# Where the rows that TensorE streams and the ring of weights begin in SBUF: another placement modulo 128 bytes in a hybrid SSD and attention layer

## The reference, cut to what matters

```
proj = x @ w_in                                        # gates | z | xBC | dt | q_a | kv_a
SSD:  conv(width 4) + SiLU on xBC, Mamba-2 scan (32 heads, 8 groups, state 128), y * silu(z), RMSNorm, @ w_ssm_proj
MLA:  q = RMSNorm(q_a) @ w_q_b, latent keys, chunk-causal softmax attention (16 heads), @ w_mla_proj
mix = (sigmoid(g_ssm) * y_ssm + sigmoid(g_mla) * y_mla) @ w_out
h = LN1(ALPHA * x + mix)
y = LN2(ALPHA * h + relu(h @ w_up)**2 @ w_down)        # w_up 1024 x 4096, w_down 4096 x 1024
```

## The kernel before

| operand | start of row k before | start of row k with the change |
|---|---|---|
| `whi`, `wlo` blocks (512 bytes each) | 0 | 64 |
| `xh`, `xl`, `q_h`, `q_l`, `ckv_h`, `ckv_l`, `o_h`, `o_l`, `mix_h`, `mix_l`, `ff_h`, `ff_l` (rows of 1152 bytes) | 64 | 0 |
| `yn` high rows (rows of 1168 bytes) | 64 + 16k | 16k |
| `e_h` | 64 + 8k (rows of 1160 bytes) | 0 (rows of 1280 bytes) |
| `e_l` | 8k | 0 |
| other tiles between `xh` and `cm` | 64, mostly | 0, mostly |

## Time and profile before

### The profile page before, as it was taken

One profiled execution on the slowest core, in us unless ns is written; L12 is line 12 of the kernel. 1 busy time (PEld: TensorE's weight loads), 2 busy tenths in 40 slices (PEclk: granted clock), 3 DMA queues, 4 the chain that ended last, 5 costly groups with the idle time before them and its releaser, 6 DMA issues.

```text
span 821.8 us, 15721 instructions
## 1 busy us (share of the span) xinstructions
PE 800.4 (97%) x6359; PEld 768.0 (93%) x6359; DVE 590.9 (72%) x980; ACT 478.9 (58%) x833; POOL 86.2 (10%) x174
## 2 busy tenths in 40 slices
PE   8999999999999999899999999999999999999994
PEld 7998999999899898799999999999999999999993
DVE  5996946836746759798888988675688887655554
ACT  5883854845755668644566545434457887633432
POOL 0223112111111002000000000000000000001212
PEclk9999999999999999999999999999999999999998
DMA  8557445335335234343444444655545555555531
GB/s 302 167 172 270 129 130 154 107 130 169 109 106 178 78 106 143 103 141 123 129 148 139 137 136 128 224 159 173 156 154 159 175 155 166 168 158 175 157 127 59
DMA packets 34809, 123.33 MB, mean 150 GB/s; under 512 B 4272, under 2 KB 4928, under 8 KB 34480
## 3 DMA queue, kind: packets, MB, share of 16 engines
q1 hardware_dynamic: 30960, 109.49, 42.8%
q0 software_dynamic: 3008, 10.98, 3.9%
q10 hardware_dynamic: 768, 1.84, 0.6%
HBM read 118.26 MB, written 4.04 MB: 149 GB/s over the span
## 4 chain that ended last, share of the span: by engine, by line
PE 70%; DVE 15%; ACT 9%; issue 3%; DMA 2%; ACTq 0%; DVEq 0%
PE ps_acc L436 12%; PE ps_acc L437 11%; PE ps_acc L438 11%; DVE wlo L1325 4%; PE ps_row L437 3%; PE ps_row L438 3%; PE ps_row L436 3%; ACT whi L936 2%; PE ps_cb L437 2%; PE ps_tr L437 2%; PE ps_tr L438 2%; PE ps_cb L438 2%; PE ps_tr L436 2%; PE ps_cb L436 2%; DVE seg L1610 2%
## 5 line engine op out<-in xcount | busy, mean ns | idle before, releaser
L1325 DVE TENSOR_TENSOR wlo<-wraw,whi 128x1024 fp32r<-128x1024 f32 x203 | 247.2, 1220 | 162.6 <-ACT whi L936 161.8
L936 ACT CAST whi<-wraw 128x1024 fp32r<-128x1024 f32 x203 | 212.3, 1046 | 126.3 <-DMA wraw<-in_wst 126.0
L436 PE MATMUL ps_acc<-xh,whi 128*128 128x288 f32 x560 | 170.9, 305 | 1.7 <-DVE mixm L1670 1.1
L437 PE MATMUL ps_acc<-xl,whi 128*128 128x288 f32 x560 | 165.2, 295 | 0.0
L438 PE MATMUL ps_acc<-xh,wlo 128*128 128x288 f32 x560 | 165.0, 295 | 0.0
L436 PEld LDWEIGHTS ps_acc<-xh,whi 128*128 128x128 f32 x560 | 105.3, 188 | 9.8 <-issue 7.2
L437 PEld LDWEIGHTS ps_acc<-xl,whi 128*128 128x128 f32 x560 | 105.4, 188 | 0.5
L438 PEld LDWEIGHTS ps_acc<-xh,wlo 128*128 128x128 f32 x560 | 105.3, 188 | 0.0
L1382 DVE SCALAR_TENSOR_TENSOR cv<-xp,vec,cv 128x292 f32<-128x292 f32 x96 | 50.2, 522 | 7.9 <-ACT cv L998 5.5
L436 PE MATMUL ps_acc<-o_h,whi 128*128 128x288 f32 x128 | 39.5, 308 | 0.0
L437 PE MATMUL ps_acc<-o_l,whi 128*128 128x288 f32 x128 | 37.8, 295 | 0.0
(11 more groups left out here) (461 smaller groups left out, 2305.4 us busy)
## 6 DMA issues: line engine op xcount, KB each, us to landing
wraw<-in_wst SPq DMA_DIRECT2D x203, 512.0 KB, 3.6
side<-in_ukT POOLq DMA_DIRECT2D x8, 256.0 KB, 4.0
side_v<-in_ukT POOLq DMA_DIRECT2D x8, 256.0 KB, 3.7
out_ssm<-s_out POOLq DMA_DIRECT2D x8, 256.0 KB, 2.5
x<-in_xT ACTq DMA_DIRECT2D x4, 288.0 KB, 4.7
ax<-in_xT POOLq DMA_DIRECT2D x1, 1152.0 KB, 6.1
out_y<-d SPq DMA_DIRECT2D x4, 288.0 KB, 2.1
ckvT<-in_cacheT POOLq DMA_DIRECT2D x1, 1024.0 KB, 7.2
```

What stands on the lines that cost most here:

```text
L436: pe.matmul(out, w, mh, start=first, stop=False)
L437: pe.matmul(out, w, ml, start=False, stop=False)
L936: act.copy(whi[:, s % RING, :], wraw[:, s % RING, :]).then_inc(split_hi, 1)
L1325: tt(wlo[:, s % RING, :], wraw[:, s % RING, :], whi[:, s % RING, :].bitcast(F32), ALU.subtract).then_inc(split_lo, 1)
```

## The change

The placement is made with steps of 128 bytes: `base`, `here` and every float32r tile. The ring (`wraw`, `wlo`, `whi`) begins HELD = 64 bytes behind a multiple of 128. `e_h` and `e_l` get rows of EW = 320 columns, of which the up stage still streams the first 290. No instruction is added, removed or moved on any engine; the shapes of all are the same. The last tile now ends 2 KB further up.

```diff
--- before.py
+++ after.py
@@ -36,6 +36,8 @@
 XW = 296
 
 RING = 5
+LINE = 128
+HELD = 64
 PIECES = 4
 WARM = 6
 CK = 1024
@@ -54,6 +56,7 @@
 N_DOWN = N_UP + FB
 N_ALL = N_DOWN + 4 * KB
 E = T + 2
+EW = T + 32
 UB = 6
 
 
@@ -157,7 +160,7 @@
                   o_y, o_ckv, o_kpe, o_ssm, o_conv):
     ctx = ExitStack()
     with ctx:
-        base = (nc.sbuf_base + 31) // 32 * 32
+        base = (nc.sbuf_base + LINE - 1) // LINE * LINE
         end = [0]
 
         def at(name, shape, off, dt=F32):
@@ -169,15 +172,16 @@
             return nc.alloc_sbuf_tensor_at(name, shape, dt, offset=base + off)
 
         def after(name, shape, dt=F32):
-            return at(name, shape, (end[0] + 31) // 32 * 32, dt)
+            line = LINE if dt == F32R else 32
+            return at(name, shape, (end[0] + line - 1) // line * line, dt)
 
         def here():
-            return (end[0] + 31) // 32 * 32
-
-
-        wraw = at("wraw", [P, RING, CK], 0)
-        wlo = at("wlo", [P, RING, CK], 0, F32R)
-        whi = after("whi", [P, RING, CK], F32R)
+            return (end[0] + LINE - 1) // LINE * LINE
+
+
+        wraw = at("wraw", [P, RING, CK], HELD)
+        wlo = at("wlo", [P, RING, CK], HELD, F32R)
+        whi = at("whi", [P, RING, CK], end[0], F32R)
         vec = after("vec", [P, V_ALL])
         con = after("con", [P, C_ALL])
         pick = after("pick", [P, HEADS_SSM], F32R)
@@ -287,8 +291,8 @@
         ff_h = at("ff_h", [P, FB, T], Z_XC, F32R)
         assert end[0] <= Z_O
         ff_l = at("ff_l", [P, FB, T], Z_A, F32R)
-        e_h = after("e_h", [P, KB, E], F32R)
-        e_l = after("e_l", [P, KB, E], F32R)
+        e_h = after("e_h", [P, KB, EW], F32R)
+        e_l = after("e_l", [P, KB, EW], F32R)
         lnt = after("lnt", [P, 2, 6, T])
         lxb = after("lxb", [P, 2, T])
         ff = after("ff", [P, 2, T])
@@ -897,7 +901,7 @@
                 for k in range(KB):
                     if b == 0:
                         pe.wait_ge(e_lo, k + 1)
-                    mm = passes(out[:, 0:E], *part(("u", b), k), e_h[:, k, :], e_l[:, k, :], k == 0, k == 7)
+                    mm = passes(out[:, 0:E], *part(("u", b), k), e_h[:, k, 0:E], e_l[:, k, 0:E], k == 0, k == 7)
                 mm.then_inc(chunk_used, 1)
 
             pe.wait_ge(gb_lo, 2)
```

## The result

| | before | with the change |
|---|---|---|
| median | 823.87 us (20 runs, 822.95 to 824.84) | 824.82 us (20 runs, 823.96 to 828.52) |
| ratio | | 1.0015, 95% interval 1.0009 to 1.0021 |
| the profiled execution | 823.72 us, span 821.8 | 824.78 us, span 822.9 |

What follows compares the result with a forecast made beforehand. The prediction took TensorE as the bound outside the SSD groups, which DVE and ACT hold; seven gains summed to 14.6 us, from 823.63 to 809.0 us, 1.8% faster, with a range of 803 to 816 us.

Steps and rivals of the forecast that it cites:

- What bounds the kernel: Whole kernel: TensorE, busy 97% at full clock, alone sets the time outside the SSD groups and latents' norms.
- the price of a matmul with the change: Dense stages: 127.7 ns instead of 132.2, counted as 4.6 gained; `w_up` 129.3 instead of 134.6, counted as 5.1.
- 0.85 ns per line of 128 bytes: Every matmul: the values' excess of 6.8 ns over eight lines, so nine lines, 7.7 ns, for a 1152-byte row.
- the exchange of keys and values: Key and value products: they change places, keys to 113.5 ns and values to 117.
- all seven terms of the sum: Gains by stretch, stage or group: 0.8 + 4.1 + 0.8 + 0.6 + 0.9 + 3.9 + 3.5 = 14.6 us.
- The two bounds, 3.3 and 5.4 ns: Gain per dense matmul: 3.3 ns gives 813.2 us for the kernel, 5.4 ns gives 807.1 us.
- the kin of the second rival: All stages: operand distance modulo 128 counts, 64 before and after, so 822.5 us; shares the second rival's chance, 0.09.
- the second rival: Only lines of 16 bytes count; only `w_up` gains, 134.6 to 133.0 ns, 1.2 us, 822.5 us; chance 0.09.
- The third rival: Dense stages: rows on a multiple of 128 are slow, 2.5 ns a matmul, 7.3 us lost, 831 us; chance 0.09.
- The bound behind the bound: `w_up`: DVE-ACT hand-over sets the pace once TensorE takes 129 ns; 3.9 us lost, 812.9 us; chance 0.07.
- The SSD groups: DVE and ACT hold the 25.66 us period; at most 0.12 us gained in each, 0.8 us in all.
- The wait of the third turn for `btok`: SSD groups, TensorE at line 747: the wait grows from 0.3 to about 0.8 us a group.

Runs made afterwards that it cites:

- e3: Kernel before with only the rows of `e_h` and `e_l` widened to 320 columns; 824.56 us, ratio 1.001.
- e15: Kernel before with 320-column rows, `e_h` at 32 and `e_l` at 0 from the weights, `ff_l` 32 below `ff_h`, modulo 256; 820.03 us, ratio 0.9956.
- e5: TensorE alone, no layer: keys' and values' products rebuilt at other distances and steps, and 64 placements of 288-column rows modulo 128; 755.04 us.
- e1: TensorE alone, no layer, DVE and ACT idle: 63 groups varying columns, starts of rows and weights, and row steps; 453.64 us.
- e13: TensorE alone, no layer: 288 and 290 columns, high and low rows' starts from 0 to 224 modulo 256, 128 groups; 875.03 us.
- e7: The change with the ring on a multiple of 128 (HELD = 0), so distance 0 from rows to weights; 825.75 us, ratio 1.0029 against before.
- the five grids: Five TensorE-alone runs without the layer, over starts of rows and, in one, low weights; 755.04, 784.49, 874.8, 875.03 and 875.9 us.
- e14: The same 128 groups as e13 in a shuffled order; 875.9 us.
- e9: Kernel before with 320-column rows, `e_h` at 32, `e_l` at 0, and low rows of most other dense stages at 32, modulo 128; 822.56 us, ratio 0.9989.
- e11: Kernel before with 320-column rows, `e_h` at 32, `e_l` at 0 modulo 128, and `ff_l` 96 above `ff_h` modulo 256; 823.31 us, ratio 0.9997.
- e2: The same 63 groups as e1, with DVE and ACT copying 128x1024 tiles beside TensorE; 453.32 us.

## Why the prediction was wrong

**What bounds the kernel** was right. TensorE has no idle time in the same stretches, and every gain or loss per matmul there arrived in the time: the sums from the table give +1.0 us for the change (0.95 measured), +1.1 for e3 (0.8 from its ratio) and -3.4 for e15 (-3.6).

**The step that failed is the price of a matmul with the change**: "What differs is which side lies on the multiple of 128", and the 0.85 ns per line of 128 bytes drawn from it. Keys and values differ in a second thing that I called alike: the steps of their rows and blocks, 1152 and 512 bytes against 1024 and 1152. e5 shows that the sides can be exchanged without effect (113.3 and 113.3) and that the speed goes with those steps. The forecast 127.7 in `w_down` came out as 132.2, the 129.3 in `w_up` as 135.35, and the exchange of keys and values did not take place (116.95 and 114.53 against 113.5 and 117 forecast). With the price at nothing, all seven terms of the sum fall together. The two bounds, 3.3 and 5.4 ns, came from the same comparison, so they did not bound it.

The reading of 0.85 ns per line fails in e1 as well. At distance 0 the excess over a column per cycle is 12.2, 13.3 and 12.2 ns at 256, 288 and 320 columns, so it doesn't grow with the lines of a row. And since even 192 columns take 111.5 ns, the values' 113.5 can't be split into 106.7 for columns and a rest that longer rows would pay on top.

**The right account was the kin of the second rival**: the distance of the operands is 64 before and after, modulo 128 (modulo 256 it is 192 before and 64 after, which 288 columns don't tell: 132.2 for both in e13). I gave it up with one sentence, "The keys and the values have the same distance, and differ", which took distance for the only thing that can count if it counts. Where distance and steps stay, the pace stayed to 0.03 ns (`xh/xl`, `w_down`). The rival's time, 822.5 us, was off too: it had mending the rows of `w_up` gain 1.2 us by lines of 16 bytes, and it lost 0.66 to 1.1. That rule of the Trainium skill (SBUF — State Buffer, specifications) is not the account here: in e1 starts of 16, 32, 48 and 0, all on such a line, cost 131.7, 134.5, 132.2 and 133.3 ns, though starts off a line, at 4 and 8, were indeed slow (135.3, 134.4).

**The third rival**, a row on a multiple of 128 as the slow one, is refuted as it was put (`w_down` stays at 132.2); what it saw in the earlier trace rows, 0.14 against 0.13 us, was `w_up`'s irregular pace. **The bound behind the bound** never came into play: `w_up` runs at 131.1 in e15, its chunks 3.15 us apart, so down to there DVE and ACT keep up; 129 ns was never reached.

**The SSD groups** were right in what holds them. Their period is 25.66 us before and 25.67 with the change:

```profile
424.36 1.75 DVE L1614 TENSOR_TENSOR seg<-seg,ps_cb 128x1536 f32<-128x1536 f32 x1
...
450.03 1.75 DVE L1614 TENSOR_TENSOR seg<-seg,ps_cb 128x1536 f32<-128x1536 f32 x1
```

and in e7, where the projection's matmuls take 0.7 ns more, 426.02 to 451.68, 25.66 us again. So matmul pace doesn't reach the period, as forecast, if shown only for a small slowing and never for the forecast gain. The wait of the third turn for `btok` is 3.4 us in eight, against 2.2 in seven, without a faster TensorE; it was no good sign to look for.

```profile
  DVE btok L1602: 3.4, 8
```

**What the moved starts do to DVE** was forecast at nothing, and is nothing: splits with a median of 1225 ns against 1224, taps 523 against 523.

```profile
L1329 DVE TENSOR_TENSOR wlo<-wraw,whi x203: 1159/1225/1253, 10.1 to 797.9; 128x1024 fp32r<-128x1024 f32 x102
```

```profile
L1386 DVE SCALAR_TENSOR_TENSOR cv<-xp,vec,cv x96: 514/523/550, 42.4 to 317.9; 128x292 f32<-128x292 f32 x96
```

**`yn`**, counted as nothing with 0.4 us either way, lost 0.14.

**What stays open.** Why the pace depends on these rests: no run shows what the two streams meet at in the memory. That a placement has two paces suggests a rhythm into which the streams fall, but that is argued, not shown. One thing speaks for it: the paces come in steps. In 409 of the 535 groups of the five grids the last 24 intervals add up to a whole multiple of 26.7 ns (64 columns at a column per cycle) within 2 ns, where chance would give some 80; 131.1, 132.2, 133.3 and 134.4 ns are 118, 119, 120 and 121 of them. Why distance 64 helps the values by 5.6 ns only together with their steps is as open. Nearly all groups were run with steps of 1152 and 1280 bytes. The low weights' place was not tried modulo 256, nor was the quick pair in the projection, which might gain 1 ns by it outside the SSD groups.

## What to carry to other kernels

Two groups of instructions that differ in speed are alike only when everything in their access patterns is, steps included; before a difference of a few ns is multiplied by thousands, rebuild one of them and change one thing at a time, for a run of groups with only TensorE in it gives some fifty such answers in 0.5 ms. When a dense float32r stream is the bound, its operands' starts and row steps are worth a grid, modulo 256 and in two orders: here the best and worst places are up to 5% apart in the grid and 3.7% in the layer's `w_up` (131.13 and 135.98 ns), and the good ones gave 0.44% of the kernel for a few lines of code.

## What the hardware showed that I had not expected

- The pace of back-to-back float32r matmuls of 288 or 290 columns depends on where the moving rows begin relative to the weights, modulo 256 bytes: 131.1 to 134.5 ns and 131.1 to 137.8 ns (e5, e13, e14).
- It depends on the low rows' place against the high ones' as well, that is on what the neighbouring matmuls read: with high rows at 64 or 192, 131.1 at 32 below and 132.8 at 96 above (e9, e11, e13).
- The same placement can run at two paces within one kernel, 133.3 or 136.7 ns, by what ran before it (e13, e14).
- Products of 256 columns with the steps of the values take 113.3 or 118.9 ns, by the distance alone (e5).
- With new weights for each matmul, 192 and 224 float32r columns both take 111.5 ns, and 64 take 111 to 113 at the full clock (e1).
- DVE and ACT at work beside it changed no steady interval by more than 0.3 ns from 192 columns on, and nearly all by less than 0.1 (e2).
